# Values' products in a split-float32 model kernel: one matmul of 512 columns and one of 256, or three of 256 from tiles at one shared offset

## What is computed

```python
proj = jnp.einsum('bsd,de->bse', h, w_in[layer])            # first block, 18432 columns
rnn_x, rnn_gate, q, k, v, attn_gate, g_rnn, g_attn = split_columns(proj)
...
u = h @ w_in                                                # second block, twice
(a_cq, a_ckv, a_kr, a_z, b_q, b_k, b_v, b_z,
 c_q, c_k, c_v, c_z, gate_logits) = jnp.split(u, SPLIT_POINTS, axis=-1)
```

## Time and profile before

| | us |
|---|---|
| median of 3 runs | 3112.68 (3112.45 to 3114.44) |
| the profiled execution | 3113.82 |
| its span, first to last instruction | 3111.6 |
| PE busy | 3090.0 (99%) |
| PE weight loads (beside the matmuls) | 2728.8 (88%) |
| DVE busy | 2128.9 (68%) |
| ACT busy | 1733.0 (56%) |
| DMA, share of 16 engines | 59.6% |

### The profile page before, as it was taken

The page is one execution under the profiler, slowest core; times in us unless marked ns, Lnnn a source line. Parts: engine busy times, 40 slices in busy tenths (PEclk is TensorE's granted clock), DMA queues, the critical chain, the costliest instruction groups (busy, mean ns, idle before and its releaser), DMA issues.

```text
span 3111.6 us, 52092 instructions
## 1 busy us (share of the span) xinstructions
PE 3090.0 (99%) x18230; PEld 2728.8 (88%) x18230; DVE 2128.9 (68%) x2741; ACT 1733.0 (56%) x2291; POOL 0.2 (0%) x4
## 2 busy tenths in 40 slices
PE   9999999999999999999999999999999999999999
PEld 7888888888888788988888888888888888888888
DVE  7677576666667687766766656777776676665675
ACT  5685444444445556656555555645665656555563
POOL 0000000000000000000000000000000000000000
PEclk9999999999999999999999999999999999999999
DMA  7656665555556555565556666566556555666555
GB/s 233 194 173 201 203 189 167 184 180 173 187 167 213 181 170 166 159 199 177 176 175 195 186 183 186 183 201 189 162 159 202 174 178 173 194 190 183 182 184 181
DMA packets 569813, 571.73 MB, mean 184 GB/s; under 512 B 26352, under 2 KB 565488, under 8 KB 569712
## 3 DMA queue, kind: packets, MB, share of 16 engines
q1 hardware_dynamic: 567440, 568.24, 59.4%
q10 hardware_dynamic: 2272, 2.18, 0.2%
HBM read 568.25 MB, written 2.10 MB: 183 GB/s over the span
## 4 chain that ended last, share of the span: by engine, by line
PE 94%; DVE 2%; ACT 2%; issue 1%; DMA 0%; SPq 0%; ACTq 0%; DVEq 0%
PE pg L533 89%; PE pa L777 1%; PE pa L794 1%; DVE hl L1288 1%; PE pa L784 1%; PE pa L533 1%; ACT hl L939 1%; PE pa L750 1%; PE pa L795 1%; PE pa L707 0%; PE pa L885 0%; DMA raw<-w_o 0%; DVE gat L1376 0%; DVE mix L1823 0%; SPq L452 0%
## 5 line engine op out<-in xcount | busy, mean ns | idle before, releaser
L533 PE MATMUL pg<-hT,hl 128*128 128x512 f32 x11456 | 1996.3, 334 | 1.5 <-DVE hl L1288 1.2
L533 PEld LDWEIGHTS pg<-hT,hl 128*128 128x128 f32 x11456 | 1729.9, 188 | 229.8 <-DVE hl L1288 3.4
L1288 DVE TENSOR_TENSOR hl<-raw,hl 128x1024 fp32r<-128x1024 f32 (+1 forms) x1071 | 1255.0, 1210 | 296.8 <-ACT hl L939 288.7
L939 ACT ACTIVATE hl<-raw 128x1024 fp32r<-128x1024 f32 (+1 forms) x1071 | 1085.2, 1044 | 293.2 <-PE pg L533 273.8
L533 PE MATMUL pg<-uT,hl 128*128 128x256 f32 (+1 forms) x3712 | 628.9, 331 | 16.0 <-DVE hl L1493 7.8
L533 PEld LDWEIGHTS pg<-uT,hl 128*128 128x128 f32 x3712 | 553.9, 189 | 86.5 <-issue 16.0
L947 ACT ACTIVATE corr<-pg 128x512 f32<-128x512 f32 x286 | 170.2, 595 | 818.3 <-PE pg L533 818.3
L533 PE MATMUL pg<-hl,hT 128*128 128x512 f32 (+1 forms) x1792 | 318.5, 336 | 0.0
L533 PEld LDWEIGHTS pg<-hl,hT 128*128 128x128 f32 x1792 | 274.6, 188 | 38.6
L1295 DVE TENSOR_TENSOR work<-pg,corr 128x512 f32<-128x512 f32 (+1 forms) x154 | 105.8, 687 | 293.8 <-ACT corr L947 293.4
L1120 ACT ACTIVATE work<-work,sm 128x256 f32<-128x256 f32 (+3 forms) x144 | 69.3, 482 | 131.3 <-DVE sm L1566 129.3
(11 more groups left out here) (191 smaller groups left out, 1371.2 us busy)
## 6 DMA issues: line engine op xcount, KB each, us to landing
raw<-w_in SPq DMA_DIRECT2D x791, 512.0 KB, 4.7
raw<-w_br SPq DMA_DIRECT2D x96, 512.0 KB, 4.3
raw<-w_out SPq DMA_DIRECT2D x64, 512.0 KB, 4.9
raw<-w_rnn SPq DMA_DIRECT2D x32, 512.0 KB, 4.8
raw<-w_o SPq DMA_DIRECT2D x32, 512.0 KB, 5.0
raw<-w_att SPq DMA_DIRECT2D x16, 512.0 KB, 4.0
raw<-w_uq SPq DMA_DIRECT2D x16, 384.0 KB, 3.7
tab<-tabs SPq DMA_DIRECT2D x5, 896.0 KB, 7.5
```

Source lines behind the costliest of these rows:

```text
L533: return nc.tensor.matmul(out, lhsT, rhs, start=start, stop=stop, skip_group_check=True)
L939: nc.scalar.activation(part(j, 0, h, 0, n), raw[:, bass.ds(j % 2 * UC + a, n)], ACT.Copy)\
L1288: tt(part(j, 1, h, 0, n), raw[:, bass.ds(j % 2 * UC + a, n)], part(j, 0, h, 0, n).bitcast(F32), ALU.subtract).then_inc(lo_done, 1)
```

## The change

`token_major` no longer uses the wide form after the first k of a chunk. For each further pair (k, s) it issues three matmuls of 256 columns: high activations by high weights, high activations by low weights, low activations by high weights. The first k of each chunk keeps the old two, since it opens the PSUM bank. The `side` order no longer applies to values. In `hl` values' units are placed apart from the others: their high and low parts both begin at 112 modulo 128, while the other weights stay at 16 and 32. `hl` grows to 8736 floats, so that what is declared behind it moves by 320 floats; `hT` would begin at 32 modulo 128 instead of 96. As a values' unit now lies a little across the place of the halves of an ordinary unit, `hi` of an ordinary unit that follows a values' unit in its slot waits for both halves of that unit (`behind_v`).

```diff
-HI_AT, LO_AT, SLOT, HL = 16, UC + 32, 2 * UC + 128, 4 * UC + 224
+HI_AT, LO_AT, SLOT, HL = 144, UC + 288, 2 * UC + 256, 4 * UC + 544
+V_SHIFT = (32, 48)
...
+            first = j % 2 * SLOT + (LO_AT if e else HI_AT) - V_SHIFT[e] * v + h * UC // 2 + a
...
-            def token_major(b, hiw, both, op, ks, start, stop, base, side):
-
-                return in_order(
-                    ks, 2, side,
-                    lambda k, s: mm(pg3[:, b + s, :], op[:, k, s * P:s * P + P], both[k - base], start and k == ks[0], False),
-                    lambda k, s: mm(pg3[:, b + s, S:], op[:, k, S + s * P:S + s * P + P], hiw[k - base], False,
-                                    stop and k == ks[-1]))
+            def token_major(b, hiw, low, both, op, ks, start, stop, base):
+
+                for k in ks:
+                    for s in range(2):
+                        xh, xl = (op[:, k, a + s * P:a + s * P + P] for a in (0, S))
+                        if start and k == ks[0]:
+                            mm(pg3[:, b + s, :], xh, both[k - base], True, False)
+                        else:
+                            mm(pg3[:, b + s, 0:S], xh, hiw[k - base], False, False)
+                            mm(pg3[:, b + s, S:], xh, low[k - base], False, False)
+                        ins = mm(pg3[:, b + s, S:], xl, hiw[k - base], False, stop and k == ks[-1])
+                return ins
...
-            def hi(u0, j, halves=(0, 1), n=UC // 2):
+            def hi(u0, j, halves=(0, 1), n=UC // 2, v=False, behind_v=False):
...
-                        act.wait_ge(half_done, 2 * (u0 + j) + h - 3)
+                        act.wait_ge(half_done, 2 * (u0 + j) + (1 if behind_v else h) - 3)
...
-                        hi(u, n + 2, halves)
+                        hi(u, n + 2, halves, v=is_v(kind, n + 2), behind_v=is_v(kind, n) and not is_v(kind, n + 2))
```

More of the change, by code:

```diff
@@ L116, in units, with is_v @@
     return UNITS[kind]
+def is_v(kind, n):
+    return n in {"1": range(12, 18), "A": (), "B": (4, 5), "C": (4, 5)}[kind]
 def chunk_of_unit(kind):
@@ L215, in build, with part @@
         pa = ctx.enter_context(nc.psum_tensor("pa", [P, 4 * 512], F32))
-        def part(j, e, h, a=0, n=UC // 2):
-            first = j % 2 * SLOT + (LO_AT if e else HI_AT) + h * UC // 2 + a
+        def part(j, e, h, a=0, n=UC // 2, v=False):
+            first = j % 2 * SLOT + (LO_AT if e else HI_AT) - V_SHIFT[e] * v + h * UC // 2 + a
             return hl[:, first:first + n]
@@ L533, in mm, with split_view @@
                 return nc.tensor.matmul(out, lhsT, rhs, start=start, stop=stop, skip_group_check=True)
-            def split_view(j, n):
-                return [[part(j, e, k * n // (UC // 2), k * n % (UC // 2), n) for k in range(UC // n)] for e in range(2)]
+            def split_view(j, n, v=False):
+                return [[part(j, e, k * n // (UC // 2), k * n % (UC // 2), n, v) for k in range(UC // n)] for e in range(2)]
             def in_order(ks, subs, side, wide, narrow):
@@ L582, in both_view @@
                     h, a = k * n // (UC // 2), k * n % (UC // 2)
-                    first = j % 2 * SLOT + HI_AT
-                    pair = hl[:, first:first + 2 * (LO_AT - HI_AT)].rearrange("p (e n) -> p e n", e=2)
+                    first, apart = j % 2 * SLOT + HI_AT - V_SHIFT[0], LO_AT - V_SHIFT[1] - HI_AT + V_SHIFT[0]
+                    pair = hl[:, first:first + 2 * apart].rearrange("p (e n) -> p e n", e=2)
                     views.append(pair[:, :, h * UC // 2 + a:h * UC // 2 + a + n])
@@ L613, in unit @@
                     base, first, last = 0, True, True
-                wh, wl = split_view(j, CH)
+                wh, wl = split_view(j, CH, form == "t")
                 if form == "r":
@@ L631, in unit @@
                         elif form == "t":
-                            ins = token_major(b, wh, both_view(j, CH), op, ks, begin, end, base, side)
+                            ins = token_major(b, wh, wl, both_view(j, CH) if first else None, op, ks, begin, end, base)
                         else:
@@ L856, in pair @@
                         cc = n // 2
-                        is_v = (kind == "1" and 6 <= cc < 9) or (kind in "BC" and cc == 2)
-                        unit(u + n, n, c + cc, cc, h3, n % 2 == 0, n % 2 == 1, "t" if is_v else "f", halves=halves,
+                        unit(u + n, n, c + cc, cc, h3, n % 2 == 0, n % 2 == 1, "t" if is_v(kind, n) else "f", halves=halves,
                              side=SIDE[kind].get(n, ()))
@@ L935, in hi @@
                     if not (isinstance(u0, int) and u0 + j < 2):
-                        act.wait_ge(half_done, 2 * (u0 + j) + h - 3)
+                        act.wait_ge(half_done, 2 * (u0 + j) + (1 if behind_v else h) - 3)
                     act.wait_ge(raw_landed[j % 2][h], landed)
                     a = h * UC // 2
-                    nc.scalar.activation(part(j, 0, h, 0, n), raw[:, bass.ds(j % 2 * UC + a, n)], ACT.Copy)\
+                    nc.scalar.activation(part(j, 0, h, 0, n, v), raw[:, bass.ds(j % 2 * UC + a, n)], ACT.Copy)\
                         .then_inc(hi_done, 1)
@@ L1155, in pair @@
                         if kind in "BC" and j == 3 and what == "u":
-                            hi(u, 5, (0,))
+                            hi(u, 5, (0,), v=True)
                             act.wait_ge(evac_done, c + 2 + 2)
@@ L1281, in _, with lo @@
             tt, stt = nc.vector.tensor_tensor, nc.vector.scalar_tensor_tensor
-            def lo(u0, j, halves=(0, 1), n=UC // 2):
+            def lo(u0, j, halves=(0, 1), n=UC // 2, v=False):
                 for h in halves:
@@ L1287, in lo @@
                     a = h * UC // 2
-                    tt(part(j, 1, h, 0, n), raw[:, bass.ds(j % 2 * UC + a, n)], part(j, 0, h, 0, n).bitcast(F32),
+                    tt(part(j, 1, h, 0, n, v), raw[:, bass.ds(j % 2 * UC + a, n)], part(j, 0, h, 0, n, v).bitcast(F32),
                        ALU.subtract).then_inc(lo_done, 1)
@@ L1645, in pair @@
                         if kind in "BC" and j == 3 and what == "u":
-                            lo(u, 5, (0,))
+                            lo(u, 5, (0,), v=True)
                             dve.wait_ge(sq_hi, pi - 4 * l - 8 + 1)
@@ L1649, in pair @@
                             halves = (1,)
-                        lo(u, n + 2, halves)
+                        lo(u, n + 2, halves, v=is_v(kind, n + 2))
                         if kind in "BC" and j == 7 and what == "u":
```

## The result

| | before | after |
|---|---|---|
| median, us | 3112.71 | 3124.32 |
| profiled span, us | 3111.6 | 3123.2 |
| PE busy, us | 3090.0 | 3096.4 |
| weight loads, count | 18230 | 19070 |

The changed kernel takes 1.0036 times as long, with a 95% interval of 1.0026 to 1.0047: **11.6 us slower**, where 5.8 us less were forecast, and outside the range. One of the seven executions of the kernel before took 3859.56 us, and the ratio is of the others. The loss splits in two nearly equal parts.

The account below looks back on a forecast made before the run. The prediction took TensorE, busy 99% of the span, as the bound. Only the cheaper threes counted, at -5.8 us, all other terms being 0: 3112.7 - 5.8 = 3106.9 us, range 3101.0 to 3119.5.

Parts of the forecast that it names:

- The bound and the prices before: TensorE's matmul steps set the time; a feature-major pair costs 340.0 ns, a values' pair 346.9 ns.
- Part (1): Values' products: 840 pairs become threes at 340.0 instead of 346.9 ns, saving 5.8 us.
- The bound taken from branch A: Twelve short matmuls in branch A's keys and values step at 117.5 ns; threes at 352.5 would cost +4.7 us.
- The guess of whole units of 6.7 ns: Stalls above 320 ns: 3 units per feature-major pair, 4 per values' pair, 5 per three short matmuls.
- the first rival: Every chain of short matmuls costs 117.5 ns wherever its tiles lie: +4.7 us, 3117.4 us; chance 0.24.
- Part (5): Longer wait before `hi` for units 18 and 19 of block 1, 6 and 7 of B and C: taken as 0.
- The shift of 1.0 us: In branch B, ACT's first high part of unit 6 moves 1.0 us later, delaying the work queued behind it.
- The cover at unit 7: In branch B, unit 7's first half is ready 1.2 us before TensorE asks; 1.0 of that is used.
- The upper bound of 2.4 us: Cost of the longer wait if the cover at unit 7 is gone: 8 x 0.3 us.
- Parts (2) to (4): 56 opening pairs at new offsets, 840 further loads and matmuls issued, dropped `side` order of values: no separate cost taken.
- The shift of `hT`: Rival: moved addresses change each feature-major pair by 6.7 ns, 49 us either way; chance 0.08. Forecast itself expected no change.
- a quarter of 0.44: Share of the likeliest case, threes at 340.0 ns with chance 0.44, counted as measurably faster; written as 0.12.

Follow-up runs that it names:

- the first table: Separate kernel that copies x and times 47 stretches of 48 matmuls, one thing changed at a time; chains of 256 columns stepped at 113.3 to 120.0 ns.

## Why the prediction was wrong

**The bound and the prices before** held. TensorE's steps set the time, 340.0 and 346.9 ns a pair came back in later runs (340.0 and 347.1 in the first table, L97 and L106), and threes in a row took 353.3 where branch A had given 352.5.

**Part (1), the price of the threes, is the first failed step.** It was read off the record of a single short matmul between two wide ones and carried over to short ones in a row because the relation of the two offsets was the same. For that one matmul the reading was right: in the feature-major stretch before, the starts are 226 and 114 ns apart in turn. But the relation doesn't carry it over: with the same 80 floats between the loaded and the moving tile, a chain that moves from 96 and loads from 16 steps at 117.9 (L75 of the first table), and one at 112 and 32 at 113.3 or at 117.8. The step of 113.3 exists in a row at exactly that place, but it depends on what ran before, and the opening pairs that the change keeps lead into the other one; so do the matmuls of the norm and the scores, which stand ahead of units 5, 16 and 17. The bound taken from branch A, 117.5 ns, lies within 0.3 of the measured 117.8. The guess of whole units of 6.7 ns for each form did not hold as a property of the form: the old pair itself went from 346.9 to 353.3 at 112. That a further weight load as such costs 6 ns, the first rival, was right in size and wrong in reason.

**Part (5), the wait taken as 0, is the second.** The shift of 1.0 us was about right: in the changed kernel ACT's first high part of unit 6 starts 5.92 us after unit 4 does, against 4.73 before, 1.2 us later. The cover at unit 7 (1.2 us) held as well. What was missing is what lies behind it on DVE. DVE works without a gap from the norm's products through the rotation, the low parts and into the first head's scores; from there the work passes from DVE to ACT and back (maxima, exponentials, sums, high parts, low parts), each waiting for the other. The norm's products start at 1391.77 in place of 1387.39 us, 4.38 later, and the second head's probabilities, 30 us on, at 1421.47 in place of 1417.13, still 4.34 later, while TensorE's own stretch there is only 3.43 later (1418.77 against 1415.34). So of about 0.9 us that the two engines were behind nothing faded, and it arrived at transposes with a cover of 0.31 us. The gaps of DVE on the way (1.93 us ahead of each RECIPROCAL, 1.4 us ahead of two low parts) absorbed nothing, since they are waits for ACT, which was as late. The list of what is queued was stopped at the first cover that was large enough. It should have been followed to a wait for TensorE's products that ends later than the shifted work, and each consumer on the way checked. The upper bound of 2.4 us stands against 5.8 in the trace and 6.0 in the run with the wait alone.

**Parts (2) to (4)** were right in being small, except that the 56 opening pairs, priced at nothing by themselves, decided the price of the 464 threes of units 12 to 15 and 4; the other 376 step at 117.8 without them too. **The shift of `hT`** did nothing, as forecast: 65.28 us for the stretch of 384.

**The rivals.** The first had 0.24 and gave +4.7 us; with the wait's 5.8 us it would have given 3123.2, near the result. Each loss alone lies within the range. Its upper end, 3119.5, does add the two, but with 2.4 us for the wait. Among the chances one sum is off: a quarter of 0.44 is 0.11 and not 0.12.

## What to carry to other kernels

A wait that is moved by 1 us has to be followed down each queue, and across to the engines that it exchanges work with, until a wait for something unshifted absorbs it; what it costs is set by the smallest cover on the way, not by the first. The price of a matmul in a new order can't be taken from its record in an old one: time the new sequence as it will stand, with the matmuls ahead of it, in a small kernel of its own; here that gave the kernel's steps, once its opening pairs stood ahead, to a nanosecond.

## What the runs showed of the hardware

At a granted clock of 1.00 a chain of matmuls with 256 columns, each with its weight load, steps at 113.3 to 120.0 ns, depending on where in 64 floats the moving and the loaded tile begin. Of the four places in steps of 16 two (16 and 48 of 64, with loads at 32) have two possible steps, 113.3 and 117.8; a chain keeps the one into which the matmuls before it lead, in the kernel over 192 matmuls (21.76 us for units 12 to 15 without the opening). Why is not settled. That it has to do with reads of the two operands meeting in SBUF is argued from the dependence on addresses alone. The Trainium skill, page "TensorE: Matmul & The Clock Gate", section "Step-by-step: what each phase is for", has the two on ports of their own, so that a load takes nothing from the running matmul. The chains that move from 96 and load from 16 or from 32, 117.9 and 119.8 ns with equal work (L75 and L76 of the first table), disagree with it, though what the two share is not shown.
